# Row maxima as a 97th row of the score product, rotary halves summed on GpSimd, and a position transform written in sequence

## The reference, cut to what matters

```python
q = einsum('bsr,rn->bsn', rmsnorm(c_q, q_norm_g), w_uq)   # 8 heads x (64 + 32)
q_nope, q_rope = q[..., :64], q[..., 64:]
q_rope = apply_rope(q_rope, cos, sin)     # x1*cos - x2*sin | x2*cos + x1*sin
k_rope = apply_rope(k_rope, cos, sin)     # one key part shared by all heads
s = einsum(q_nope, k_nope) + einsum(q_rope, k_rope)
p = softmax(s * scale)                    # over the 512 keys
o = einsum('bhqk,bkhd->bqhd', p, v)
f = fftn(ug, axes=(1, 3), norm='ortho').real   # positions and 128 channels
```

## Time and profile before

| | |
|---|---|
| median of 3 runs | 1408.82 us (1408.48 to 1410.33) |
| the profiled execution: its time | 1408.91 us |
| its span, first to last instruction | 1407.1 us |
| mean granted TensorE clock | 0.997 |
| busy: PE / PEld / DVE / ACT / POOL | 1369.9 / 1148.0 / 832.6 / 668.9 / 832.2 us |

### The profile page before, as it was taken

The page is one execution under the profiler, slowest core; times in us unless marked ns, Lnnn a source line. Parts: engine busy times, 40 slices in busy tenths (PEclk is TensorE's granted clock), DMA queues, the critical chain, the costliest instruction groups (busy, mean ns, idle before and its releaser), DMA issues.

```text
span 1407.1 us, 18114 instructions
## 1 busy us (share of the span) xinstructions
PE 1369.9 (97%) x6560; PEld 1148.0 (82%) x6560; DVE 832.6 (59%) x1020; ACT 668.9 (48%) x1236; POOL 832.2 (59%) x631
## 2 busy tenths in 40 slices
PE   8999999999999999999999899999999999999997
PEld 6977789888898778888888688888888888878776
DVE  3666547143456574551636875666666565488966
ACT  5576646445336774663546423333333233444355
POOL 4758758731445776694146755555554553477884
PEclk9999999999999999999999999999999999999999
DMA  8401054514322103463143133333323326963234
GB/s 280 167 27 34 24 180 143 157 38 135 99 65 90 45 9 101 143 190 99 61 138 132 60 131 102 105 113 112 103 93 112 112 83 222 322 218 113 83 98 157
DMA packets 101032, 165.17 MB, mean 117 GB/s; under 512 B 8784, under 2 KB 42960, under 8 KB 100944
## 3 DMA queue, kind: packets, MB, share of 16 engines
q1 hardware_dynamic: 100944, 164.02, 35.7%
HBM read 135.41 MB, written 28.57 MB: 117 GB/s over the span
## 4 chain that ended last, share of the span: by engine, by line
PE 86%; DVE 5%; POOL 4%; ACT 2%; issue 2%; DMA 0%; SPq 0%; ACTq 0%; DVEq 0%
PE ps L1977 27%; PE ps L1979 26%; PE ps L1978 26%; POOL w_lo L763 2%; PE ps L2152 1%; PE ps L2155 1%; PE ps L2154 1%; PE ps L2153 1%; PE ps L2132 1%; DVE w_lo L1399 1%; DVE act_lo L1399 1%; ACT junk L940 1%; DVE x_res L1519 1%; POOL h_lo_P L763 0%; POOL wd L900 0%
## 5 line engine op out<-in xcount | busy, mean ns | idle before, releaser
L763 POOL TENSOR_TENSOR w_lo<-w_raw,w_hi 128x512 fp32r<-128x512 f32 (+2 forms) x236 | 308.7, 1323 | 224.1 <-ACT w_hi L918 223.5
L1977 PE MATMUL ps<-h_hi_P,w_hi 128*128 128x512 f32 x616 | 241.3, 392 | 4.3 <-issue 2.1
L1978 PE MATMUL ps<-h_lo_P,w_hi 128*128 128x512 f32 x616 | 240.5, 390 | 0.0
L1979 PE MATMUL ps<-h_hi_P,w_lo 128*128 128x512 f32 x616 | 240.3, 390 | 0.0
L918 ACT ACTIVATE w_hi<-w_raw 128x512 fp32r<-128x512 f32 (+2 forms) x236 | 140.7, 607 | 198.8 <-PE ps L1979 172.6
L763 POOL TENSOR_TENSOR w_lo<-w_sum,w_hi 128x512 fp32r<-128x512 f32 x88 | 118.3, 1348 | 115.9 <-ACT w_hi L918 115.9
L763 POOL TENSOR_TENSOR w_lo<-a_raw,w_hi 128x512 fp32r<-128x512 f32 x77 | 111.9, 1455 | 74.2 <-ACT w_hi L918 74.2
L1977 PE MATMUL ps<-w_hi,act_hi 128*128 128x512 f32 (+2 forms) x384 | 140.7, 366 | 1.5 <-POOL w_lo L763 1.5
L1977 PEld LDWEIGHTS ps<-h_hi_P,w_hi 128*128 128x128 f32 x616 | 116.0, 188 | 30.6 <-issue 4.1
L1979 PE MATMUL ps<-w_hi,act_lo 128*128 128x512 f32 (+2 forms) x384 | 139.9, 364 | 0.0
L1978 PE MATMUL ps<-w_lo,act_hi 128*128 128x512 f32 (+2 forms) x384 | 139.8, 364 | 0.0
(11 more groups left out here) (255 smaller groups left out, 3017.5 us busy)
## 6 DMA issues: line engine op xcount, KB each, us to landing
gu_raw<-in_w_gate_up SPq DMA_DIRECT2D x22, 1024.0 KB, 5.7
a_raw<-a_mem SPq DMA_DIRECT2D x77, 256.0 KB, 2.7
w_raw<-in_w_xkv SPq DMA_DIRECT2D x64, 256.0 KB, 3.2
a_mem<-down_sum SPq DMA_DIRECT2D x44, 256.0 KB, 2.6
wd<-in_w_down SPq DMA_DIRECT2D x44, 256.0 KB, 6.0
a_mem<-act_t SPq DMA_DIRECT2D x33, 256.0 KB, 2.1
w_raw<-in_w_out SPq DMA_DIRECT2D x32, 256.0 KB, 2.6
w_raw<-in_w_xq SPq DMA_DIRECT2D x32, 256.0 KB, 2.9
```

The costliest lines, as they stand in the source:

```text
L763: return nc.gpsimd.tensor_tensor(out, whole, hi.bitcast(F32), ALU.subtract)
L1977: nc.tensor.matmul(out, s_hi, m_hi, start=start, stop=False, skip_group_check=more)
L1978: nc.tensor.matmul(out, s_hi, m_lo, start=False, stop=False, skip_group_check=more)
L1979: return nc.tensor.matmul(out, s_lo, m_hi, start=False, stop=stop, skip_group_check=more)
```

## The change

The fourth score product goes. Queries and keys shrink to 96 rows (64 plain, 32 rotary) and get a 97th: the keys' is a row of minus ones (the key tile `k_st` brings them), the queries' is the row of their maxima. To turn the maxima into a row, PE multiplies each of the four columns of maxima with the identity (`turned_maxima`, new), and ScalarE copies the row from PSUM into row 96 of the rounded query (`row_out`, new). The last of the three score products then runs over 97 rows and stands last, since the row comes late. VectorE's diagonal goes.

The two rotary parts of a query are no longer added by the product: VectorE multiplies them in two operations into `q_turn` and `q_f`, and GpSimd adds the 32 rows (`query_turned`, new) before ScalarE can round the query. VectorE makes the query of head h+2 before the copy of finished values. ScalarE copies the sums one block earlier. The position transform is read from PSUM with a step of 128 elements and written in sequence.

```diff
@@ constants, tables
-        minus_ones = at("minus_ones", 69.5, [P, P], F32R)
+        ident_r = at("ident_r", 69.5, [P, P], F32R)
+        top = at("top", 69.125, [P, 2 * T], F32R)
...
-        turn = at("turn", R + 0, [P, 2, S])
+        turn = at("turn", R + 0, [P, S])
+        q_turn = at("q_turn", R + 2, [P, S])
@@ GpSimd
-                for i in range(4):
-                    nc.gpsimd.tensor_tensor(k_st[:, :, i, 0:HALF], k_rot[:, 0], k_rot[:, 1],
-                                            ALU.subtract).then_inc(krot.sem, 1)
...
+                nc.gpsimd.memset(k_st[:, :, 1, :], -1.0).then_inc(krot.sem, 1)
...
+            def query_turned(g, h):
+                pool.wait_ge(*free(g, f"Q{h}"))
+                nc.gpsimd.tensor_tensor(q_f[NOPE:DQ, :], q_f[NOPE:DQ, :], q_turn[NOPE:DQ, :], ALU.add).then_inc(q_rot.sem, 1)
+                pool.wait_ge(q_rot.sem, q_rot.at(g, h + 1))
...
+                pool.wait_ge(v_filled.sem, v_filled.at(g, 2))
+                query_turned(g, 0)
                 query_lo(g, 0)
+                pool.wait_ge(q_lo.sem, q_lo.at(g, 1))
+                query_turned(g, 1)
...
+                        if b == 3 and h + 2 < HEADS:
+                            pool.wait_ge(p_lo.sem, p_lo.at(g, T * h + b))
+                            query_turned(g, h + 2)
                         prob_lo(g, T * h + b)
@@ ScalarE
             def query_hi(g, h):
...
-                act.wait_ge(*free(g, f"Q{h}"))
-                copy(qt_hi[:, h % 2, :], q_f[:]).then_inc(q_hi.sem, 1)
+                act.wait_ge(q_rot.sem, q_rot.at(g, h + 1))
+                copy(qt_hi[0:DQ, h % 2, :], q_f[0:DQ, :]).then_inc(q_hi.sem, 1)
+
+            def row_out(g, h):
+                act.wait_ge(a_full.sem, a_full.at(g, 3 * h + 3))
+                copy(qt_hi[DQ:DQ + 1, h % 2, :], ps[0:1, A_BANK, :]).then_inc(max_row.sem, 1)
...
-                    hi_out(g, ten, act_hi[:, 4 + c, :].rearrange("p (n k) -> p k n", k=ROOT),
-                           tile4(ten))
+                    hi_out(g, ten, act_hi[:, 4 + c, :].rearrange("p (n k) -> p n k", k=ROOT),
+                           tile4(ten).rearrange("p k n -> p n k"))
...
-                        if b == 2 and h >= 1:
+                        if b == 1 and h >= 1:
                             sums_out(g, h - 1)
...
+                        if b == 2 and h + 1 < HEADS:
+                            row_out(g, h + 1)
@@ VectorE
-                nc.vector.tensor_tensor(q_f[:], ps[:, Q_BANK, :], turn[:, h % 2, :], ALU.mult).then_inc(psum_free.sem, 1)
+                nc.vector.tensor_tensor(q_turn[NOPE:DQ, :], ps[DQ:P, Q_BANK, :], turn[DQ:P, :], ALU.mult)
+                nc.vector.tensor_tensor(q_f[0:DQ, :], ps[0:DQ, Q_BANK, :], turn[0:DQ, :], ALU.mult).then_inc(psum_free.sem, 1)
...
-            def head_diag(g, h):
...
+                if g == 0:
+                    nc.vector.tensor_copy(ident_r[:], ident[:])
                 query_out(g, 0)
@@ PE
+            def turned_maxima(g, h):
+
+                pe.wait_ge(a_max.sem, a_max.at(g, 2 * h + 2))
+                o = h % 2 * T
+                for t in range(T):
+                    last = nc.tensor.matmul(ps[0:1, A_BANK, t * P:(t + 1) * P], top[:, o + t:o + t + 1], ident_r[:],
                                             start=True, stop=True)
                 last.then_inc(a_full.sem, 1)
...
-                    pe.wait_ge(diag.sem, diag.at(g, h + 1))
-                nc.tensor.matmul(out, kt_hi[:, j, o], qt_hi[:, j, :], start=True, stop=False)
...
-                nc.tensor.matmul(out, minus_ones[:], max_diag[j].rearrange("p t q -> p (t q)"),
+                nc.tensor.matmul(out, kt_hi[0:DQ, j, o], qt_lo[0:DQ, j, :], start=True, stop=False)
+                nc.tensor.matmul(out, kt_lo[0:DQ, j, o], qt_hi[0:DQ, j, :], start=False, stop=False)
+                if b == 0:
+                    pe.wait_ge(max_row.sem, max_row.at(g, h + 1))
+                nc.tensor.matmul(out, kt_hi[0:DQ + 1, j, o], qt_hi[0:DQ + 1, j, :],
                                  start=False, stop=True).then_inc(b_full.sem, 1)
...
+                        if b == 2 and h + 1 < HEADS:
+                            row_maxima(g, h + 1, 1)
                         scores(g, h, b)
+                        if b == 1 and h + 1 < HEADS:
+                            row_maxima(g, h + 1, 0)
...
+                        if b == 2 and h + 1 < HEADS:
+                            turned_maxima(g, h + 1)
```

More of the change, by code:

```diff
@@ L73, in constant_tables @@
     rotation = np.concatenate([np.cos(angles), sign * np.sin(angles)]).astype(f)
-    ones = np.ones((P - 2 * rope_dim, seq), dtype=f)
-    turn = [np.concatenate([ones, rotation]), np.concatenate([rotation, ones])]
+    turn = [np.concatenate([np.ones((P - 2 * rope_dim, seq), dtype=f), rotation])]
     return np.ascontiguousarray(np.concatenate([np.eye(P, dtype=f), cos, sin, dft, chan] + turn, axis=1))
@@ L84, in query_columns @@
     swapped = np.roll(rope, rope_dim // 2, axis=2)
-    even = np.concatenate([nope, rope, swapped], axis=2)
-    odd = np.concatenate([rope, swapped, nope], axis=2)
-    return np.ascontiguousarray(np.stack([even[:, 0::2], odd[:, 1::2]], axis=2).reshape(rows, -1))
+    return np.ascontiguousarray(np.concatenate([nope, rope, swapped], axis=2).reshape(rows, -1))
 def key_value_columns(w_ukv, heads, nope_dim):
@@ L258, in build @@
         y_n = at("y_n", R + 84, [P, 2, S])
-        max_diag = [act[:, PAIRS - 1, :].rearrange("p (t q) -> p t q", q=P) for act in (act_hi, act_lo)]
         kx_hi = at("kx_hi", R + 0, [P, KD, M], F32R)
@@ L371, in build @@
         kr_lo = Count(sem("kr_lo"), 2)
-        a_full = Count(sem("a_full"), 2 * HEADS)
+        a_full = Count(sem("a_full"), 3 * HEADS)
         a_max = Count(sem("a_max"), 2 * HEADS)
-        diag = Count(sem("diag"), HEADS)
+        max_row = Count(sem("max_row"), HEADS)
+        q_rot = Count(sem("q_rot"), HEADS)
         q_hi = Count(sem("q_hi"), HEADS)
@@ L967, in key_rope_hi @@
                 for j in range(2):
-                    copy(kt_hi[half_rows(1 - j), j, :], ps[half_rows(1 - j), A_BANK, :]).then_inc(kr_hi.sem, 1)
+                    copy(kt_hi[NOPE:P, j, :], ps[0:P - NOPE, A_BANK, :]).then_inc(kr_hi.sem, 1)
             def query_hi(g, h):
@@ L979, in key_hi @@
                 act.wait_ge(*full(g, f"K{h // 2}"))
-                o = half_rows(h % 2)
-                copy(kt_hi[o, h % 2, :], ps[o, K_BANK, :]).then_inc(k_hi.sem, 1)
+                copy(kt_hi[0:NOPE, h % 2, :], ps[half_rows(h % 2), K_BANK, :]).then_inc(k_hi.sem, 1)
             def value_hi(g, t):
@@ L1606, in _ @@
                 head_max(g, 0, 1)
-                head_diag(g, 0)
                 for t in range(1, T):
@@ L1615, in _ @@
                         key_lo(g, h + 1)
+                    if h + 1 < HEADS:
+                        head_max(g, h + 1, 0)
                     if h >= 3 and h % 2 == 1:
@@ L2069, in key_rope @@
             def key_rope(g):
-                pe.wait_ge(krot.sem, krot.at(g, 12))
+                pe.wait_ge(krot.sem, krot.at(g, 7))
                 pe.wait_ge(psum_free.sem, psum_free.at(g, TEN["cq"] + 2))
                 for t in range(T):
-                    last = nc.tensor.transpose(ps[:, A_BANK, t * P:(t + 1) * P],
+                    last = nc.tensor.transpose(ps[0:2 * ROPE, A_BANK, t * P:(t + 1) * P],
                                                k_st[:, t].rearrange("p a d -> p (a d)"), ident[:])
@@ L2127, in row_maxima @@
                     pe.wait_ge(psum_free.sem, psum_free.at(g, TEN["cq"] + 3))
-                if h > 0 or half > 0:
-                    pe.wait_ge(a_max.sem, a_max.at(g, 2 * h + half))
+                if half > 0:
+                    pe.wait_ge(a_max.sem, a_max.at(g, 2 * h + 1))
+                elif h > 0:
+                    pe.wait_ge(max_row.sem, max_row.at(g, h))
                 for i in range(2):
                     t = 2 * half + i
-                    last = nc.tensor.matmul(ps[:, A_BANK + i, :], qt_hi[:, h % 2, t * P:(t + 1) * P], kt_hi[:, h % 2, :],
+                    last = nc.tensor.matmul(ps[:, A_BANK + i, :], qt_hi[0:DQ, h % 2, t * P:(t + 1) * P],
+                                            kt_hi[0:DQ, h % 2, :], start=True, stop=True)
+                last.then_inc(a_full.sem, 1)
+            def turned_maxima(g, h):
[3 more added lines that the diff above has]
+                    last = nc.tensor.matmul(ps[0:1, A_BANK, t * P:(t + 1) * P], top[:, o + t:o + t + 1], ident_r[:],
                                             start=True, stop=True)
```

54 lines of the change are left out of this document (19 added, 35 removed).

## The result

The changed kernel takes **1413.93 us** (median of 7 runs, 1413.44 to 1416.66) against 1408.81 for the kernel before in the same session (7 runs, 1407.84 to 1411.74): a ratio of 1.0038, 95% interval 1.0028 to 1.0048. It is slower by 5.1 us; the prediction was 1412.9 within 1407.0 to 1418.5, with a chance of 0.63 for more than 1411.6. The profiled execution took 1413.78 us with a span of 1412.0 and a mean granted clock of 0.999.

A forecast was written before the change was run, and what follows sets the result against it. PE was taken to bound the kernel, with GpSimd's queue deciding locally; the first group's 2.1 us and the second's 1.9 add 4.0 to the profiled 1408.91, giving 1412.9 us, range 1407.0 to 1418.5.

The forecast's parts named there:

- W8: Mark on PE, first group: weighted values of block 8, forecast at 121.7 against 118.37, 3.3 us late.
- W24: Mark on PE, first group: weighted values of block 24, forecast at 160.45 against 157.78, 2.7 us late.
- W31: Mark on PE, first group: weighted values of block 31, forecast at 177.5 against 175.38, 2.1 us late.
- Step 1: Start of head 0's row maxima: faster position transform is spent by the longer query chain, 84.4 against 84.28, 0.1 late.
- Rival B: Position transform gets no faster, strided PSUM reads costing what strided SBUF writes did: 1.9 us a group, 1416.7; chance 0.17.
- term for a set: Four one-column products turning maxima into a row on PE: 0.57 us a set, 9.1 us in all for 16.
- Rival C: One-column products cost the f32 price, 0.20 rather than 0.12 us: 1.9 us a group, 1416.7; chance 0.18.
- PE's own balance: PE alone: 14.5 us of score products saved, 9.1 us of sets added, a gain of 5.4 us, not forecast.
- Steps 2 and 3: First group: scores of block 0 at 92.4 instead of 91.40; then GpSimd's first subtraction of a block at 98.6 instead of 96.02.
- Rival D: GpSimd's 32x512 addition is short, 0.55 us instead of 1.25: 2.8 us a group saved, 1407.3; chance 0.13.
- Step 4: Heads 0 and 1: GpSimd's queue of 18 operations instead of 16 up to block 8 makes W8 3.3 us late.
- Step 5: W8 to W24: PE leads until block 2 of head 5, then GpSimd's queue; W24 at 160.45, 2.7 us late.
- Step 6: W24 to W31: 17.60 us before, less five products (1.13), plus a set (0.57); W31 2.1 us late.

The follow-up runs named there:

- the version that won: Kernel before with the change, the sum on VectorE, query 1, late row maxima, small products and first row copy reordered: 1400.42 us, ratio 0.9937.

## Why the prediction was right, and where it was not

| mark, first group | before | predicted | after |
|---|---|---|---|
| gate | 84.28 | 84.4 | 84.38 |
| scores 0 | 91.40 | 92.4 | 92.11 |
| GpSimd's first rest of a block | 96.02 | 98.6 | 98.44 |
| W8 | 118.37 | 121.7 | 121.83 |
| W24 | 157.78 | 160.45 | 161.43 |
| W31 | 175.38 | 177.5 | 178.32 |

**Step 1, the gate: right in its parts.** That the sum comes within 0.02 is luck, as the gate alone moves by 1.7 between executions. VectorE in the changed kernel:

```profile
77.55 2.48 DVE L1411 TENSOR_TENSOR act_lo<-ps,act_hi 128x512 fp32r<-128x512 f32 x4
79.95 0.21 DVE L1603 CAST ident_r<-ident 128x128 fp32r<-128x128 f32 x1
80.32 0.69 DVE L1459 TENSOR_TENSOR q_turn<-ps,turn 32x512 f32<-32x512 f32 x1 [0.15 <-PE ps L1983]
81.03 0.69 DVE L1460 TENSOR_TENSOR q_f<-ps,turn 96x512 f32<-96x512 f32 x1
```

The four subtractions take 2.48 instead of 4.00, 0.62 each, and the longer query chain spends what they give back; the part alone gains 1.55 a group. **Rival B falls**: a read of PSUM by strides of 512 bytes costs nothing here (0.62, against 0.63 in sequence), while writing SBUF by strides of 16 bytes cost VectorE 0.38 on each operation. The rule that the prediction weighed (the Trainium skill, SBUF — State Buffer, section on the DMA port swizzle) agrees with the rows for the write; for PSUM it names matmuls as what its smaller lines slow, and VectorE's read shows no price.

**The term for a set was mis-sized: 0.57, measured 0.29.** The set at 89.74 and the product behind it at 89.97 give 0.23 for four products, 0.058 each, below the bound of 0.07; with the longer first step behind it 0.29:

```profile
89.74 0.40 PE L2147 MATMUL ps<-ident_r,top 128*1 128x128 f32 x4
89.97 0.44 PE L1981 MATMUL ps<-c_hi,w_hi 128*128 128x512 f32 x1
```

**Rival C falls** with it. PE's own balance would have been 14.5 less 16 x 0.29, a gain of 9.9 instead of 5.4. That twice the gain did not make the time faster is what the prediction's choice of bound was about: other queues decided.

**Steps 2 and 3: right.** The chain that step 3 added up puts the first rest of a block at 98.44: VectorE's two products (92.31 and 93.01), GpSimd's sum (93.84), ScalarE's rounding, which waits for it, the table load, exponential and rounding. PE's three start-up waits lie beside this chain.

```profile
95.16 0.63 ACT L925 ACTIVATE qt_hi<-q_f 96x512 fp32r<-96x512 f32 x1 [4.26 <-POOL q_f L798]
```

**Rival D falls.** The line of the sum, ns min/median/max: 32x512 takes what 128x512 takes.

```profile
L798 POOL TENSOR_TENSOR q_f<-q_f,q_turn x16: 1274/1282/1293, 81.9 to 527.7; 32x512 f32<-32x512 f32 x16
...
who waited for it (us, times):
  ACT qt_hi L925: 27.9, 16
```

The rule of cores with their own partitions (the Trainium skill, GPSIMD Engine Reference, Instruction dispatch) agrees.

**Step 4, W8: the size right within 0.13, the wait wrong.** The prediction let PE wait at W8 for the rest of block 8. That rest was ready at 121.4, as its count gave, but PE was not waiting for it: it had stood 1.08 us at 117.76 for query 3, whose sum lies 13 operations down the same queue. The prediction named this in a sentence ("Behind the addition, ScalarE's next query rounding waits") without a price. The two runs on single rests tell the two apart; taking an operation away behind the sum, as step 4 would have had it, gains nothing. Of the 3.4 us by which W8 lies further behind the gate than before (37.45 against 34.09), 2.3 are there when GpSimd's run begins (14.06 against 11.74): the longer chain of the first queries, which step 3 had priced. The other microsecond comes behind that point.

**Step 5, W24: the queue that sets it right, its start 1.0 too early, and PE's waits in other places.** As forecast, GpSimd's queue is the longer way to W24: from the rest of block 23 it takes 5.05 (156.38 to 161.43), and took 5.09 before (152.69 to 157.78). But the forecast let that rest begin behind the addition for query 7 at 155.3, and the addition itself began only at 155.01, held by VectorE:

```profile
155.01 1.28 POOL L798 TENSOR_TENSOR q_f<-q_f,q_turn 32x512 f32<-32x512 f32 x1 [0.65 <-DVE q_f L1460]
156.38 1.28 POOL L760 TENSOR_TENSOR pt_lo<-prob,pt_hi 128x512 fp32r<-128x512 f32 x1
```

VectorE's products for query 7 (153.47 and 154.18) follow the second maximum, and that follows the slow scaling without a gap (150.08 to 154.87, shown above). The scaling was costed at nothing. PE, forecast to wait over a microsecond at W24, waited only 0.18 there, as it began block 2 of head 5 some 0.4 later than forecast (150.31) and lost more in small waits for VectorE and ScalarE behind it (0.42 at 153.50, 0.31 at 157.74, 0.72 at 159.85). The scaling's line in the kernel before and in the changed one (ns min/median/max):

```profile
L1491 DVE TENSOR_TENSOR y_n<-y_raw,y_n x8: 669/681/1560, 126.5 to 551.0; 128x512 f32<-128x512 f32 x8
```

```profile
L1493 DVE TENSOR_TENSOR y_n<-y_raw,y_n x8: 691/1380/2226, 130.1 to 556.6; 128x512 f32<-128x512 f32 x8
```

In heads 3 and 5 of both groups it took 2.07 to 2.23, and 0.67 in the kernel before; the other four of the changed kernel took 0.69. That it is what held W24 is read from the trace; the run that moved it did not take its cost away. Heads 2 to 4 (W8 to W20) became faster by 0.26 each, not 0.5; with the sum on VectorE it is 0.4.

**Step 6 and the sum.** W24 to W31 took 16.89 against a forecast of 17.05, the second group lost 2.68 against 1.9. Sets that cost half of their price (4.5 us in all) were given back in waits that had no price, and the sum came within 1.0 us of the median. The size of the total is therefore partly luck; its sign is not, as the run with the sum on VectorE and a kept queue shows.

## What to carry to other kernels

Before a short operation is given to an engine, count what stands ahead of it in that engine's queue, when that queue starts, and who waits for its result: an operation of 1.28 us whose consumer is on the path cost the whole queue ahead of it here, while one behind that consumer's operand cost nothing. Price each moved piece alone if it can be run alone; here one part of the change gained 3 us and the others lost 8 in the same launch. When a wait is taken away, look at every in-order queue that the value passes through (PE, VectorE and ScalarE were reordered together in the version that won), for a piece moved on one engine only has moved the wait.

## What was not expected of the hardware

- VectorE's multiplication of two SBUF tiles of 128x512 took between 0.69 and 2.23 us in the changed kernel; the four long ones began while GpSimd was in a run of subtractions without a gap, and each ended 0.54 to 0.56 us behind the end of that run (152.31 against 151.76 in head 5). In the kernel before, it took 0.67 at 126.45, and GpSimd's subtraction that began at 126.80 took 1.48 instead of 1.29. The Trainium skill (SBUF — State Buffer, section "Who interferes with whom") has a VectorE instruction with two SBUF inputs contend with a GpSimd instruction that reads SBUF, over a shared read port that is locked to one of the two, and lets the order of issue decide which of them is blocked. The row of before agrees with it; the long ones waited not for one instruction but for the rest of the run (at 150.08 for the subtraction in progress and for the one that began at 150.47). No run here isolates it.
- GpSimd's operation on 32 partitions took 1.03 us where both inputs were the same tile, 1.28 where they were two.
- The same wait of 1.62 us on PE was followed by half the granted clock until about 97.5 us in one group of an execution and by full clock in the other; its price was 1.4 us. In the run without the row a wait of 1.60 was followed by full clock in the first group, one of 1.62 by half the clock in the second, for 1.9 us.
